# Layer 1 of a fused three-layer kernel: its four attention heads and eight recurrence tails get other step numbers

## The reference, cut to what matters

```python
def rglru(x, w_a, b_a, w_x, b_x, lam):           # 16 blocks of 128 columns
    r = sigmoid(einsum(xb, w_a) + b_a); i = sigmoid(einsum(xb, w_x) + b_x)
    log_a = -8 * r * softplus(-lam)
    a = exp(log_a)
    u = sqrt(-expm1(2 * log_a)) * (i * x)
    h = scan over positions of  a * h + u

def mlstm(q, k, v, ig, lf):                      # 4 heads, value width 512
    sc  = (q k^T) * exp(dmat - m)                # causal
    den = sum(sc) + ...; num = sc v + ...
    h = num / max(|den|, exp(-m))
    h = rmsnorm(h) * m_norm

y = concat(h_lru, o * h_mlstm) * silu(z)
x = x + y @ w_out
```

## Time and profile before

| | us |
|---|---|
| runs, median of 3 | 3267.24 |
| lowest, highest | 3265.41, 3267.34 |
| the profiled execution | 3270.49 |
| its span, first to last instruction | 3268.7 |
| PE busy in the span | 3108.3 (95%) |
| DVE busy | 2313.3 (71%) |
| ACT busy | 1837.6 (56%) |

### The profile page before, as it was taken

The page is one execution under the profiler, slowest core; times in us unless marked ns, Lnnn a source line. Parts: engine busy times, 40 slices in busy tenths (PEclk is TensorE's granted clock), DMA queues, the critical chain, the costliest instruction groups (busy, mean ns, idle before and its releaser), DMA issues.

```text
span 3268.7 us, 53596 instructions
## 1 busy us (share of the span) xinstructions
PE 3108.3 (95%) x21726; PEld 2873.6 (88%) x21726; DVE 2313.3 (71%) x3156; ACT 1837.6 (56%) x2371; POOL 541.3 (17%) x640
## 2 busy tenths in 40 slices
PE   6989898999999999998989999999999999999998
PEld 6889888888998999887878888999998888888887
DVE  6655788656777777656777788885656788888544
ACT  5554678644676676654555454445445666666443
POOL 2000000000000000112655576850001000000000
PEclk9999999999999999999999999999999999999999
DMA  5445444655555555555433344556555555555554
GB/s 201 138 140 175 149 133 135 209 188 200 170 173 172 174 171 197 178 192 194 159 107 123 129 149 136 174 167 209 186 182 193 187 190 190 190 190 189 192 188 141
DMA packets 158041, 560.50 MB, mean 171 GB/s; under 512 B 17552, under 2 KB 25808, under 8 KB 157152
## 3 DMA queue, kind: packets, MB, share of 16 engines
q1 hardware_dynamic: 157792, 557.06, 51.3%
HBM read 550.64 MB, written 6.36 MB: 170 GB/s over the span
## 4 chain that ended last, share of the span: by engine, by line
PE 75%; DVE 11%; ACT 8%; issue 2%; POOL 1%; DMA 1%; SPq 0%; DVEq 0%; ACTq 0%; POOLq 0%
PE ps L560 75%; DVE WL L1330 3%; ACT WH L907 2%; ACT L897 2%; DVE XV L1304 1%; DVE BS L1293 1%; POOL TB L1915 1%; DMA scratch<-X 0%; DVE X L1304 0%; ACT DB L897 0%; DVE BS L1320 0%; DVE XC L1304 0%; DVE XMC L1304 0%; DMA RAW<-in_w 0%; ACT RB L897 0%
## 5 line engine op out<-in xcount | busy, mean ns | idle before, releaser
L560 PE MATMUL ps<-XN,WH 128*128 128x256 f32 (+1 forms) x8864 | 1875.1, 305 | 48.8 <-DVE WL L1330 26.6
L907 ACT ACTIVATE WH<-RAW 128x1024 fp32r<-128x1024 f32 x1010 | 1065.1, 1057 | 1164.3 <-PE ps L560 1130.9
L1330 DVE TENSOR_TENSOR WL<-RAW,WH 128x1024 fp32r<-128x1024 f32 x1010 | 1257.0, 1250 | 481.1 <-ACT WH L907 474.4
L560 PEld LDWEIGHTS ps<-XN,WH 128*128 128x128 f32 x8864 | 1451.4, 194 | 126.0 <-DVE WL L1330 29.4
L560 PE MATMUL ps<-XN,WL 128*128 128x256 f32 x5120 | 1453.9, 284 | 0.0
L560 PEld LDWEIGHTS ps<-XN,WL 128*128 128x128 f32 x5120 | 990.8, 194 | 0.0
L560 PE MATMUL ps<-YS,WH 128*128 128x512 f32 (+1 forms) x1088 | 367.9, 386 | 4.7 <-DVE YS L1293 2.2
L560 PE MATMUL ps<-YS,WL 128*128 128x256 f32 x1056 | 295.2, 280 | 0.0
L1915 POOL TENSOR_TENSOR RSB<-RSB,SQ 128x256 f32<-128x256 f32 x75 | 75.9, 1012 | 1262.0 <-ACT SQ L897 1260.9
L560 PEld LDWEIGHTS ps<-YS,WH 128*128 128x128 f32 x1088 | 202.1, 188 | 48.4 <-DVE YS L1293 2.5
L560 PE MATMUL ps<-HS,WH 128*128 128x512 f32 x688 | 238.6, 392 | 0.0
(11 more groups left out here) (332 smaller groups left out, 3354.7 us busy)
## 6 DMA issues: line engine op xcount, KB each, us to landing
RAW<-in_w SPq DMA_DIRECT2D x1010, 512.0 KB, 3.3
CSB<-sums SPq DMA_DIRECT2D x64, 128.0 KB, 3.8
scratch<-X SPq DMA_DIRECT2D x2, 2048.0 KB, 7.9
X<-scratch SPq DMA_DIRECT2D x2, 2048.0 KB, 8.1
X<-in_x SPq DMA_DIRECT2D x4, 512.0 KB, 7.5
X<-in_x SPq DMA_DIRECT2D x1, 2048.0 KB, 7.9
out<-X SPq DMA_DIRECT2D x4, 512.0 KB, 2.6
WIF<-in_w_if SPq DMA_DIRECT2D x1, 576.0 KB, 13.9
```

The costliest lines, as they stand in the source:

```text
L560: return pe.e.matmul(dst, l, r, start=start, stop=stop, skip_group_check=True)
L907: act.e.activation(WH[:, w % NH, :], RAW[:, w % NB, :], ACT.Copy).then_inc(*act.one(("wh", w)))
L1330: dve.e.tensor_tensor(WL[:, w % NB, :], RAW[:, w % NB, :], WH[:, w % NH, :].bitcast(F32), SUB).then_inc(*dve.one(("wl", w)))
```

## The change

`heads` becomes 65 steps. Head h still begins at step 16h, but a head now has 17 steps, and `in_flight` gives the one or two heads that have a step at s. Steps 0 to 3 stay. The sums over the scores and all that follows stand two steps later: on PE 5 becomes 7 and 10 becomes 12; on DVE 6, 12 and 14 become 8, 14 and 16; on ACT 7, 11 and 13 become 9, 13 and 15; on POOL 8 becomes 10. A head's last step falls on the next head's step 0. `tail` gets 7 steps: DVE's subtraction goes from 1 to 2, ACT's exp of TH from 2 to 3, DVE's scans from 3 to 4, the copies from 4 and 5 to 5 and 6. Its `End` moves to just before the next pair's ra and ix blocks.

```diff
@@ -57,7 +57,7 @@
...
-    "tail": 6, "heads": 64, "eo": 1, "dt": 1, "dts": 6, "xv": 1, "zs": 1, "ssd": 20, "oo": 1, "nx": 4,
+    "tail": 7, "heads": 65, "eo": 1, "dt": 1, "dts": 6, "xv": 1, "zs": 1, "ssd": 20, "oo": 1, "nx": 4,
...
@@ -110,6 +110,8 @@
...
+        if q > 1:
+            p.append(End("tail", (q - 2,)))
...
@@ -119,8 +121,6 @@
...
-            if q:
-                p.append(End("tail", (q - 1,)))
...
@@ -683,8 +683,7 @@
...
-            def heads(s):
-                h, s = divmod(s, 16)
+            def head(h, s):
...
                 if s == 0:
...
@@ -696,7 +695,7 @@
...
-                if s == 5:
+                if s == 7:
...
@@ -708,10 +707,14 @@
...
-                if s == 10:
+                if s == 12:
...
+            def heads(s):
+                for h, r in in_flight(s):
+                    head(h, r)
...
             def dts(s):
                 if s == 4:
@@ -1040,15 +1043,14 @@
                 if s == 1:
...
-                if s == 2:
+                if s == 3:
...
-                if s == 4:
+                if s == 5:
...
-            def heads(s):
-                h, s = divmod(s, 16)
+            def head(h, s):
                 if s == 1:
...
@@ -1058,16 +1060,20 @@
...
-                if s == 7:
+                if s == 9:
...
-                if s == 11:
+                if s == 13:
...
-                if s == 13:
+                if s == 15:
...
+            def heads(s):
+                for h, r in in_flight(s):
+                    head(h, r)
...
             def eo(n, s):
...
@@ -1470,10 +1476,10 @@
                 if s == 0:
...
-                if s == 1:
+                if s == 2:
...
-                if s == 3:
+                if s == 4:
...
@@ -1481,12 +1487,11 @@
...
-                if s == 5:
+                if s == 6:
...
-            def heads(s):
-                h, s = divmod(s, 16)
+            def head(h, s):
                 if s == 1:
...
@@ -1498,7 +1503,7 @@
...
-                if s == 6:
+                if s == 8:
...
@@ -1510,14 +1515,18 @@
...
-                if s == 12:
+                if s == 14:
...
-                if s == 14:
+                if s == 16:
...
+            def heads(s):
+                for h, r in in_flight(s):
+                    head(h, r)
...
             def project(L, kind, n, load):
...
@@ -1935,10 +1944,10 @@
...
             def heads(s):
-                h, s = divmod(s, 16)
-                if s == 8:
-                    pool.wait_ge(*at("hsqr", h))
-                    halves(("hsq", h))
+                for h, r in in_flight(s):
+                    if r == 10:
+                        pool.wait_ge(*at("hsqr", h))
+                        halves(("hsq", h))
...
             def ssd(g, s):
                 if s == 13:
@@ -2109,6 +2118,11 @@
...
+def in_flight(s):
+    return [(h, s - 16 * h) for h in range(4) if 0 <= s - 16 * h < 17]
 def cols(a, n):
...

```

## The result

| | before | changed |
|---|---|---|
| median, us (6 runs each, in turn) | 3266.88 | 3278.53 |
| lowest, highest | 3265.41, 3267.67 | 3277.26, 3279.33 |
| profiled execution, its span | 3270.49, 3268.7 | 3277.26, 3275.4 |
| from the start of unit 89 to that of unit 172 | 300.2 | 308.5 |

The ratio of the medians is 1.0034, 95% interval 1.0023 to 1.0045. The forecast was 3256.2 us, a gain; it was wrong in sign.

The account below looks back on a forecast made before the run. Bound: PE, DVE and ACT close to full, losing time at handovers. -2.1 - 1.9 - 3.0 - 3.0 - 4.0 + 2.5 - 0.5 = -12.0, taken as -11 us: profiled 3259.5, median 3256.2 us; range 3247 to 3265.

Parts of the forecast that it names:

- The sums over EB: PE, two units later: all four waits for EB go; only head 0's is directly on the chain, -2.1 us.
- the rest of head 0: DVE's subtraction no longer catches ACT in the middle of TH, less what the squares take: -1.9 us.
- the signs that it is wrong: Wrong if DVE's idle time stays at 25 us, or waits for SQ grow beyond 8 us in all.
- head 1's half clock: PE after head 1's wait for EB: four us at half clock cost 2.0 us, expected to go with the wait.
- Heads 1 and 2: DVE and ACT handovers before WL: -3.0 us at each head, against +2.5 us for both from late sums of squares.
- both loads are on the chain ... so 3.5 us: Head 1, ACT: RS2's logarithm, exp and two table loads no longer stand before a WH; 3.5 us, less 0.5 handed back.
- late by 2 to 3 us at heads 1 and 2: Sums of squares reach PE late without the wait for EB; only part counts, +2.5 us for both heads.
- Head 3: PE's wait for SQ shrinks by 2.0 us to about 1.5 and the clock stays up, 2.0 us: -4.0 us.
- The boundary: Before the projection: PE's wait for ZB shortens because the gate's evacuation comes sooner; between 0 and -2, taken -0.5 us.
- Edits at nothing: Moved `End`, unchanged instruction and table-load counts, `x1` waiting on SP for head 3's `ysh`: no cost.
- POOL: POOL's sums of squares slow DVE through shared SBUF interfaces: counted 0, four clashes' 4.4 us only in the upper end.
- PE waits for SQ at every head: Slower rival, `ats` at step 12: waits and half clock at heads 1 to 3, +8.6 us, 3275.8 us; chance 0.07.

Follow-up runs that it names:

- e18: Kernel before with head 0 alone shifted (sums over EB at step 7, `ats` at 12, and so on); 3268.1 us, ratio 0.9995.
- e14: Kernel before with head 3 alone shifted (sums over EB at step 7, `ats` at 12, and so on); 3275.4 us, ratio 1.0023.
- e1: Kernel before with the heads' half of the change alone, tails keeping their six steps; 3275.8 us, ratio 1.0020.
- e2: Kernel before with the tails' half of the change alone (seven steps, `End` moved), heads as before; 3268.8 us, ratio 1.0001.
- e13: Changed kernel with head 3 alone back at the step numbers of before; 3273.1 us, ratio 1.0012.
- e6: Changed kernel with `ats` and all that follows it (RS2, norm, copies) two steps later, at 14 to 18; 3274.8 us, ratio 1.0015.
- e4: Changed kernel with heads 17 steps apart instead of 16; 3282.8 us, ratio 1.0044.
- e9: Kernel before without POOL's two additions, PE adding the four quarters of SQ itself; 3265.8 us, ratio 0.9992.
- e5: Changed kernel without POOL's two additions, PE adding the four quarters of SQ itself; 3275.5 us, ratio 1.0022.
- e11: Kernel before with DVE's products of HB not using or waiting for RS2 (mean-square scaling left out of the result); 3272.1 us, ratio 1.0010.
- e8: Changed kernel with PE also waiting for EB at step 5 as before, sums staying at step 7; 3282.0 us, ratio 1.0037.

## Why the prediction was wrong, point by point

Adding up the stretch by heads: head 0 -1.8 (e18), head 3 +6.5 (e14), heads 1 and 2 together 7.0 + 1.8 - 6.5 = +2.3 (from e1), tails +0.9 (e2): +7.9 of the 8.3 measured. Heads 1 and 2 are what is left over, for no kernel shifts one of them alone; reckoned from e13 they come to 2.5 + 1.8 - 0.9 = +3.4.

- *The sums over EB.* All four waits went, as forecast, and head 0's 2.1 us was real: 2.3 us at unit 105. The further 1.9 us for the rest of head 0 did not come (e18: -1.8 in all against -4.0). The waits of DVE for TH did go, all 4.5 us, but others took their place. DVE's waits in the changed kernel from 402 to 582 us, columns as in rows 1:

```profile
DVE WL L1336 <- ACT WH L910: 15.3, 15, 2.1
DVE IB L1299 <- ACT IB L900: 6.8, 3, 2.3
DVE YS L1299 <- ACT YS L900: 6.0, 4, 2.6
DVE HB L1310 <- ACT RS L900: 4.5, 2, 2.3
```

  The wait for WH grew from 8.8 to 15.3, the one for RS stayed (4.6, 4.5), and those for the sigmoid of IB and the copy to YS are new among the large ones. In these 180 us DVE is busy 137.7 us instead of 146.3. The text named idle time of DVE that stays, and waits for SQ above 8 us, as the signs that it is wrong; both came. The price of head 1's half clock is right for the place, but the clock falls wherever PE waits next, and no term of the sum had that.
- *Heads 1 and 2.* Forecast -3.0 - 3.0 + 2.5 = -3.5, measured +2.3. The failed step is "both loads are on the chain ... so 3.5 us": what stands in front of one WL was counted as cost there, and where it goes as nearly free ("part of the gain is handed back", 0.5 us). The row that mattered was ACT's, beside it: RS2 was made before ACT's tanh and logarithms, so DVE's products ran beside these; two steps later, at head 1, two conversions and one exp stood behind it, and then ACT waited for DVE's products itself. The waits for a bank were not in the sum at all for these heads: ZB grew by 10.1 us, more than any other wait, 5.75 of it at head 2. The wait for SQ was undersized too: "late by 2 to 3 us at heads 1 and 2" counted 2.5 together, with 17.9 us of cover against the 18.5 of before. The 18.5 contained the catch-up in PE's pause and had the scans behind the denominator; without both, the sums were ready after 24.8 and 26.5 us. Measured waits 4.30 and 1.54 us, the latter behind 5.75 us for ZB.
- *Head 3.* Forecast -4.0, measured +6.5. This is the step with the largest error, and an omission: only the wait for SQ was costed, not RS2 and the products, which move two units as well and meet the last pair. The prediction took 3.5 us for head 1 leaving the order that the earlier trace rows show, and nothing for head 3 entering it. Even the costed part failed: the wait shrank from 3.52 to 3.23, not to 1.5, and the clock fell again (0.50 from 561.3 us), because the denominator came 9.3 us after PE's sums instead of 8.5.
- *The boundary.* Forecast -0.5; 12.9 us instead of 8.1, by head 3, not by the tails (6.8 us in e2).
- *Edits at nothing.* The tails' `End` and table loads: e2 shows no more than 0.9 us for the whole half. Head 3's copy was early enough for the projection, and so it was two units later (e6, no wait for YS). Three units later (e4) it was not: PE waited 8.64 us for the copy itself, the YS that it multiplies, not for weight loads behind `x1`.
- *POOL.* Forecast 0 with 4.4 us in the upper end. e9 and e5 agree with 0 for the change. The clash itself is in both traces: a pair of scans took 2.70 us instead of 1.42 while POOL summed, and one took 2.41 us in the kernel before. That is the rule on shared SBUF interfaces in the Trainium skill (GPSIMD Engine Reference, Specifications); it does not tell the two kernels apart.
- *The rivals.* "PE waits for SQ at every head" had given 3275.8, the nearest number, and its sign and condition came true (24.8 us against 17.9). Its price was partly another's: with no such wait left (e6), 5.2 of the 8.3 us stay. It was given 0.07 although its own text said that the condition was met at two heads; with three engines at 80 to 88% busy from 402 to 582 us, a rival whose condition the rows already meet should have had the larger share.

What stays open: the 3.4 us between the 11.7 of the medians and the 8.3 of the stretch, which the interval of the medians covers; the 4.0 us between the two measures of e11; and how the +2.3 us of heads 1 and 2 divide between the late sums of squares and RS2, since each relief gave about 3 us and they were not all tried together.

## What to carry to other kernels

Where two engines hand work to each other through queues that are in step with a third, a wait of the third is time in which the other two catch up. Ask whether the third is on the chain there: here only head 0's wait for EB, which was on it, was worth its length, and those of heads 1 to 3 came back at no price (e8). Where work is repeated at a drifting distance to other work, a shift that takes one repetition out of a costly order can put another into it, so go through all of them. Of work that is moved, look at what the other engine does beside it at the old place and at the new one, for every instruction of the step to its end, the last one before a boundary above all. And judge such edits by the stretch they touch, at its end: in e13 a lag of 6.7 us in its middle was 1.3 us at unit 157 and 2.5 us at the end.

## What the runs showed of the hardware that was not expected

A wait taken away need not help at all: DVE without its 4.6 us for RS2 in the kernel before left the stretch at 300.6 against 300.2 us (its median is even 4.4 us higher, with an interval of 0.3 to 6.2). And PE adding four quarters of SQ itself, three more matmuls a head (units 89 to 104 take 53.6 instead of 52.3 us), was cheaper than two additions on POOL, together 2.1 to 3.3 us long in the changed kernel: the stretch is 3.0 and 3.8 us shorter without them (e5, e9).
